# Depthwise convolution of a two-layer encoder: the taps that TensorE summed go to ScalarE and GpSimd

## The chip, the cores and the metric

The program runs on one core of a Trainium2 chip. A core has a matrix engine (TensorE, PE in the profile), a vector engine (VectorE, DVE), an activation engine (ScalarE, ACT), a general engine (GpSimd, POOL) and a queue engine (SyncE, SP). Each runs its own list of instructions in order; they meet at semaphores. SBUF is the working memory of 128 partitions, PSUM the memory that matmuls write, in eight banks of 512 float32 columns. The metric is the device time of one execution in microseconds (us), the median of several runs.

## The reference

Two layers of a streaming encoder over 384 tokens: one prompt of 256 and eight samples of 16. Layer 0 mixes by attention and retention, layer 1 by a convolution module; behind each stands a mixture of experts. What matters here is the convolution module, on 1024 channels, all float32:

```python
def conv_glu(h, w_pw1, b_pw1):
    a, g = jnp.split(jnp.einsum('btd,dc->btc', h, w_pw1) + b_pw1, 2, axis=-1)
    return a * jax.nn.sigmoid(g)

def conv_rest(u_ext, w_dw, b_dw, ln_g, ln_b, w_pw2):
    y = lax.conv_general_dilated(u_ext, w_dw[:, None, :], ... feature_group_count=CONV_CH) + b_dw
    y = jax.nn.silu(layer_norm(y, ln_g, ln_b))
    return jnp.einsum('btc,cd->btd', y, w_pw2)
```

`u_ext` is the gated projection with 30 tokens of history in front. Each channel's output is a sum of 31 shifted copies of its input, each times one weight of that channel (a tap).

## The kernel before

The channels lie on the partitions, in eight blocks c = 0 to 7 of 128 channels; a block has 384 token columns. The tile `U[:, c]` holds a block as 24 groups of 16 tokens, each with its 30 columns of history in front, so tap w of a block is one read of `U[:, c, :, w:w+16]`, 128x384.

The stage goes like this, all written out in order by hand, with semaphores between the engines:

- PE: `glu(c)` (L925 to L938) makes both halves of the projection of block c in two PSUM banks, with the weights in the slots that SP fills. `conv_taps(c)` (L940 to L949) then sums six taps in a third bank, as matmuls with diagonal matrices `DG`. The order is glu(0), then glu(c+1) and conv_taps(c) in turn (L951 to L955). Banks go round by three for GLU, by two for taps.
- ACT: `sigmoids(c)` (L1183) makes SGC; three copies (L1200 to L1202) spread the history over `U` and take the new sample tokens to `UN`; `diagonals(c+2)` (L1186) makes the six diagonal matrices of a later block.
- DVE: `gated(c)` (L1601) multiplies both halves of the GLU into `U`. Taps 6 to 30 follow, alternately summed in two accumulators, YC and YD (L1612 to L1626), with `gated(c+1)` between them, behind the fourteenth. L1630 adds YD to YC, L1632 adds PE's six taps from PSUM; then `y_conv` is signalled.
- POOL: nothing in this stage except, once, the stores of the convolution caches, when ACT has copied them out of PSUM (`ctok_ready`).

Behind it comes a tail for all blocks: PE sums the mean (L966), DVE centres (L1636), ACT squares (L1215), PE sums the variance (L970), ACT takes the root (L1217), DVE the reciprocal (L1639) and the product (L1642), ACT applies SiLU (L1221), and PE starts the second projection (L769). PE's transposes for the caches (L959, L961) stand ahead of the mean.

`q.do` and `q.link` are DVE's and ACT's helpers: they issue an instruction with a semaphore; `link` waits for it at once, `settle` for all that is open.

Of the kernel before, what the change touches and what calls it, by code (L numbers as in the profile page):

```python
# [19 lines left out]
ALU = mybir.AluOpType  # L20
ACT = mybir.ActivationFunctionType
AXX = mybir.AxisListType.X

P = 128
D = 1024
KD = D // P
NT = 3
TOK = NT * P
SEQ, NS, LS, PAST = 256, 8, 16, 128
# [9 lines left out]
CONV_W, HIST = 31, 30  # L39
# [10 lines left out]
NEG = -1e30  # L50
NBLK = TOK // LS
PBLK = SEQ // LS
PE_TAPS = 6
UNIT = 2048
LO, HI = 6, 12
NEAR = 6
# [108 lines left out]
def build(nc, a, o):  # L165

    with ExitStack() as ctx:
        sems = {}

        def S(name):  # L170
            if name not in sems:
                sems[name] = ctx.enter_context(nc.semaphore(name))
            return sems[name]
# [118 lines left out]
        NC = over("NC", [P, NT, D])  # L292
        YC = rc("YC", [P, KD, TOK])
        YD = rc("YD", [P, TOK])
        DG = rc("DG", [P, 2, PE_TAPS, P])
        VR = rc("VR", [P, TOK])
        SGC = rc("SGC", [P, 2, TOK])
        over = Region(rc.n, limit)
        UN = over("UN", [P, KD, P])
        CC = rc("CC", [P, 2, D])  # L300
        WDR = rc("WDR", [P, D])
        WDT = rc("WDT", [P, KD, CONV_W])
        SMR = rc("SMR", [P, P])
        SMT = rc("SMT", [P, 40])
        CS = WDR
        CP = rc("CP", [P, D])

        PS = nc.alloc_psum_tensor("PS", [P, 8, 512], F32)
# [134 lines left out]
        def _(pool):  # L443
# [41 lines left out]
            for lay in range(2):  # L485

                pool.wait_ge(S("x_mixed"), 8 * (lay + 1))
                pool.dma_start(WR[:, :, 0:NG], a["w_router_group"][lay].rearrange("(p k) n -> p k n", k=KD)
                               ).then_inc(S("router_in"), 16)
                pool.dma_start(WR[:, :, NG:NR], a["w_router_expert"][lay].rearrange("(p k) n -> p k n", k=KD)  # L490
                               ).then_inc(S("router_in"), 16)
                pool.dma_start(BR[:, 0:NG], row(a["b_router_group"][lay], NG)).then_inc(S("router_in"), 16)
                pool.dma_start(BR[:, NG:NR], row(a["b_router_expert"][lay], NE)).then_inc(S("router_in"), 16)
                if lay == 0:
                    pool.wait_ge(S("hn_ready"), 2 * NT)
                    pool.dma_start(gb[:, :], row(a["norm_mix"][1], D)).then_inc(S("gain_in"), 16)
                    pool.wait_ge(S("moe_done"), 1)
                    pool.dma_start(CC[0:120, 0, :], a["cache_conv"][0, 0:4].rearrange("b t c -> (b t) c")
                                   ).then_inc(S("conv_in"), 16)
                    pool.dma_start(CC[0:120, 1, :], a["cache_conv"][0, 4:8].rearrange("b t c -> (b t) c")  # L500
                                   ).then_inc(S("conv_in"), 16)
                    pool.dma_start(WDR[0:CONV_W, :], a["w_dw"][0]).then_inc(S("conv_in"), 16)
                    pool.dma_start(SMR[0:16, :], a["b_pw1"][0].rearrange("(c p) -> c p", p=P)
                                   ).then_inc(S("conv_in"), 16)
                    for i, name in enumerate(("b_dw", "conv_ln_g", "conv_ln_b")):
                        pool.dma_start(SMR[16 + 8 * i:24 + 8 * i, :], a[name][0].rearrange("(c p) -> c p", p=P)
                                       ).then_inc(S("conv_in"), 16)
                    pool.wait_ge(S("hn_ready"), 3 * NT)
                    pool.dma_start(gb[:, :], row(a["norm_ffn"][1], D)).then_inc(S("gain_in"), 16)

                    pool.wait_ge(S("ctok_ready"), 2)
                    store(o["conv_prompt"][0, 0], CP[0:HIST, :])
                    for b in range(NS):
                        store(o["conv_sample"][0, b, HIST - LS:HIST, :], CS[LS * b:LS * (b + 1), :])
                    pool.wait_ge(S("stored"), 16 * (STATE_STORES + CONV_STORES))
# [5 lines left out]
        def _(pe):  # L521
# [400 lines left out]
            pe.wait_ge(S("hn_ready"), 3 * NT)  # L922
            transpose_stream(NC)
            wait_stream(4)
            def glu(c):  # L925
                m, cc = divmod(c, 2)
                if cc == 0:
                    full("c", 2 * m)
                    full("c", 2 * m + 1)
                if c >= 3:  # L930
                    pe.wait_ge(S("u_ready"), c - 2)
                for g in range(2):
                    w = dense(2 * m + g)
                    for k in range(KD):
                        last = mm(PS[:, 2 * (c % 3) + g, 0:TOK], w[:, k, P * cc:P * (cc + 1)], HC[:, k, :],  # L935
                                  start=k == 0, stop=k == KD - 1)
                    if g == 1:
                        last.then_inc(S("glu_done"), 1)  # L938

            def conv_taps(c):  # L940

                pe.wait_ge(S("uhist_ready"), c + 1)
                pe.wait_ge(S("diag_ready"), PE_TAPS * (c + 1))
                if c >= 2:
                    pe.wait_ge(S("y_conv"), c - 1)
                for w in range(PE_TAPS):
                    last = mm(PS[:, 6 + c % 2, 0:TOK], DG[:, c % 2, w, :], U[:, c, :, w:w + LS],
                              start=w == 0, stop=w == PE_TAPS - 1)
                last.then_inc(S("pe_taps"), 1)  # L949

            glu(0)  # L951
            for c in range(KD):
                if c + 1 < KD:
                    glu(c + 1)
                conv_taps(c)  # L955

            pe.wait_ge(S("unew_ready"), KD)
            for c in range(KD):
                nc.tensor.transpose(PS[0:HIST, c // 4, P * (c % 4):P * (c % 4 + 1)], U[:, c, PBLK - 1, LS:LS + HIST],  # L959
# [3 lines left out]

            for c in range(KD):
                pe.wait_ge(S("y_conv"), c + 1)
                last = mm(PS[:, 4, 0:TOK], C["onesd"], YC[:, c, :], start=c == 0, stop=c == KD - 1)  # L966
            last.then_inc(S("mean_done"), 1)
            for c in range(KD):
                pe.wait_ge(S("ysq_ready"), c + 1)
                last = mm(PS[:, 5, 0:TOK], C["onesd"], YS[:, c, :], start=c == 0, stop=c == KD - 1)  # L970
            last.then_inc(S("var_done"), 1)
            pe.wait_ge(S("ctok_ready"), 2)
            project_out("c", 8, YC, "pw_done", 8, "z_ready")
# [5 lines left out]
        def _(act):  # L979
# [199 lines left out]
            def sigmoids(c):  # L1179
                act.wait_ge(S("glu_done"), c + 1)  # L1180
                if c >= 2:
                    act.wait_ge(S("u_ready"), c - 1)
                q.do(A(SGC[:, c % 2, :], PS[:, 2 * (c % 3) + 1, 0:TOK], ACT.Sigmoid, bias=SMT[:, 8 + c:9 + c]),  # L1183
                     S("sig_ready"))

            def diagonals(c):  # L1186

                if c >= 2:
                    act.wait_ge(S("pe_taps"), c - 1)
                for w in range(PE_TAPS):  # L1190
                    q.do(A(DG[:, c % 2, w, :], ident, ACT.Copy, scale=WDT[:, c, w:w + 1]), S("diag_ready"))

            act.wait_ge(S("hist_tr"), KD)
            diagonals(0)
            diagonals(1)
            sigmoids(0)
            for c in range(KD):

# [5 lines left out]
                q.settle()  # L1204
                if c + 1 < KD:
                    sigmoids(c + 1)
                if c + 2 < KD:
                    diagonals(c + 2)
            act.wait_ge(S("ctok_tr"), 1)
            q.do(A(CP[0:HIST, :], PS[0:HIST, 0:2, :].rearrange("p a n -> p (a n)"), ACT.Copy), S("ctok_ready"))  # L1210
            q.do(A(CS[:, :], PS[:, 2:4, :].rearrange("p a n -> p (a n)"), ACT.Copy), S("ctok_ready"))
# [2 lines left out]
                act.wait_ge(S("yc_centred"), c + 1)  # L1214
                q.do(A(YS[:, c, :], YC[:, c, :], ACT.Square), S("ysq_ready"))  # L1215
            act.wait_ge(S("var_done"), 1)
            q.link(A(VR[:, :], PS[:, 5, 0:TOK], ACT.Sqrt, bias=C["eps"]), S("cstd_ready"))  # L1217
            preload(ACT.Silu)
            for c in range(KD):
                act.wait_ge(S("yc_normed"), c + 1)  # L1220
# [6 lines left out]
        def _(dve):  # L1227
# [370 lines left out]
            def blocks(x):  # L1598
                return x.rearrange("p (b l) -> p b l", l=LS)

            def gated(c):  # L1601

                dve.wait_ge(S("sig_ready"), c + 1)
                q.do(V.scalar_tensor_tensor(U[:, c, :, HIST:], blocks(PS[:, 2 * (c % 3), 0:TOK]), SMT[:, c:c + 1],
                                            blocks(SGC[:, c % 2, :]), ALU.add, ALU.mult), S("u_ready"))

            gated(0)
            for c in range(KD):
                dve.wait_ge(S("uhist_ready"), c + 1)

                accs, sides = (blocks(YC[:, c, :]), blocks(YD[:, :])), (S("conv_a"), S("conv_b"))
                for w in range(PE_TAPS, CONV_W):  # L1612
                    n = w - PE_TAPS
                    acc, side = accs[n % 2], sides[n % 2]
                    if side is sides[1] and n < 2 and c:
                        dve.wait_ge(S("conv_sum"), c)
# [7 lines left out]
                    else:  # L1624
                        ins = V.scalar_tensor_tensor(acc, src, tap, acc, ALU.mult, ALU.add)  # L1625
                    q.do(ins, side)  # L1626
                    if n == 13 and c + 1 < KD:
                        gated(c + 1)
                q.settle()
                q.link(V.tensor_tensor(YC[:, c, :], YC[:, c, :], YD[:, :], ALU.add), S("conv_sum"))  # L1630
                dve.wait_ge(S("pe_taps"), c + 1)
                q.do(V.tensor_tensor(YC[:, c, :], YC[:, c, :], PS[:, 6 + c % 2, 0:TOK], ALU.add), S("y_conv"))  # L1632
            q.settle()
            dve.wait_ge(S("mean_done"), 1)
            for c in range(KD):
                q.do(V.tensor_tensor(YC[:, c, :], YC[:, c, :], PS[:, 4, 0:TOK], ALU.subtract), S("yc_centred"))  # L1636
            q.settle()
            dve.wait_ge(S("cstd_ready"), 1)
            q.link(V.reciprocal(VR[:, :], VR[:, :]))  # L1639
# [33 lines left out]
```

## Time and profile before

| | us |
|---|---|
| median of 3 runs (1300.19 to 1302.35) | 1300.33 |
| the profiled execution | 1300.19 |
| its span, first to last instruction | 1298.4 |
| busy in the span: PE | 1142.4 |
| DVE | 458.5 |
| ACT | 241.7 |
| POOL | 37.5 |

The span is what the profile covers; the time of the execution has 1.8 us more around it. A busy share is an average over stages: PE stands at 88% over the whole, while the convolution, from about 728 to 890 us of the span, has shares of its own.

How the rows are read. A row of a timeline gives the start in us from the span's start, the duration in us (from the first start to the last end, if it merges several), engine, line, operation, output and inputs, the count, and in brackets how long the engine was idle before and who released it. A row of the instruction groups gives the shape and count, then the busy us in total and the mean ns of one, then the idle time before them. A row of the waits gives engine, tile and line, what it waited for, and us in total, times and longest. A row of the windows gives the stretch, its length, then for PE, PEld (weight load), DVE, ACT and POOL the busy us with the number of instructions, then the granted TensorE clock as a share of 2.4 GHz, the busy share of the DMA engines and GB/s.

### The profile page before, as it was taken

Reading aid. Unit: us, or ns where it says so; the run is one execution under the profiler, and the core shown is the slowest. Engines: PE = TensorE matmul, PEld = TensorE weight load, DVE = VectorE, ACT = ScalarE, POOL = GpSimd, SP = SyncE. Lnnn points to the kernel's source line nnn. Section 1 sums busy time; section 2 is a strip of 40 time slices with the busy share of each in tenths; the row PEclk is TensorE's granted clock in tenths of the full one; section 3 lists DMA queues with packets and bytes.
Section 4 is the critical chain, followed back from the end, with each engine's and each line's share of the span. In section 5 each row is a group of like instructions: output and inputs, shape, how many; then the busy total and the mean of one; then the engine's idle time right before and its main releaser. Section 6 shows DMA issues by size and latency. Waiting matters only on the chain. (4 is left out here: it accounts for less than half of the span.)

```text
span 1298.4 us, 15664 instructions
## 1 busy us (share of the span) xinstructions
PE 1142.4 (88%) x6307; PEld 843.0 (65%) x6307; DVE 458.5 (35%) x869; ACT 241.7 (19%) x502; POOL 37.5 (3%) x64
## 2 busy tenths in 40 slices
PE   3998895789579999999996899959759999999996
PEld 2887794568566766766663555528657666776673
DVE  1122335450422333123322499970431332133323
ACT  2005323320211111111112322131211111111110
POOL 2000000010100000000001000010000000000000
PEclk9989997569769999999998899979769999999999
DMA  9422214227108878778784123701207878787761
GB/s 274 149 65 90 65 66 171 74 61 282 54 1 346 327 284 337 276 307 325 279 313 134 34 68 107 279 20 65 70 1 323 318 272 338 298 321 289 297 258 49
DMA packets 71528, 249.48 MB, mean 192 GB/s; under 512 B 4779, under 2 KB 33571, under 8 KB 54960
## 3 DMA queue, kind: packets, MB, share of 16 engines
q1 hardware_dynamic: 68224, 239.42, 49.0%
q0 software_dynamic: 3264, 9.51, 2.8%
q8 instruction: 27, 0.44, 0.1%
q14 instruction: 13, 0.11, 0.0%
HBM read 243.93 MB, written 5.44 MB: 192 GB/s over the span
## 5 line engine op out<-in xcount | busy, mean ns | idle before, releaser
L815 PE MATMUL PS<-slot,XG 128*64 128x256 f32 x2048 | 229.0, 382 | 2.4 <-ACT XG L1125 2.4
L815 PEld LDWEIGHTS PS<-slot,XG 128*64 128x64 f32 x2048 | 146.9, 138 | 83.0 <-issue 13.7
L805 PE MATMUL PS<-G,XHI 128*128 128x256 f32 x384 | 159.6, 416 | 11.2 <-DVE G L1535 8.9
L805 PE MATMUL PS<-G,XLO 128*128 128x256 f32 x384 | 156.1, 406 | 0.0
L805 PEld LDWEIGHTS PS<-G,XHI 128*128 128x128 f32 x384 | 129.1, 336 | 11.8 <-DVE G L1535 9.2
L1570 DVE SCALAR_TENSOR_TENSOR YL<-PS,GATE,YH 128x1024 fp32r<-128x1024 f32 x32 | 41.1, 1284 | 270.0 <-ACT YH L1145 270.0
L565 PE MATMUL PS<-slot,HT 128*128 128x256 f32 x576 | 131.7, 388 | 2.9 <-ACT PJ L1014 2.2
L805 PEld LDWEIGHTS PS<-G,XLO 128*128 128x128 f32 x384 | 130.0, 338 | 0.0
L565 PEld LDWEIGHTS PS<-slot,HT 128*128 128x128 f32 x576 | 110.9, 195 | 18.9 <-issue 2.9
L838 PE MATMUL PS<-slot,HID 128*64 128x512 f32 x512 | 116.9, 598 | 6.1 <-issue 4.8
L1577 DVE TENSOR_TENSOR X<-X,PS 128x512 f32<-128x512 f32 x96 | 66.0, 687 | 104.7 <-PE PS L885 104.7
L885 PE MATMUL PS<-YH,GT 128*128 128x512 f32 x192 | 82.2, 428 | 5.7 <-DVE YL L1570 5.7
L935 PE MATMUL PS<-HC,slot 128*128 128x384 f32 x256 | 83.8, 486 | 0.7 <-ACT HC L1002 0.7
L885 PE MATMUL PS<-YL,GT 128*128 128x512 f32 x192 | 77.1, 402 | 0.0
L838 PEld LDWEIGHTS PS<-slot,HID 128*64 128x64 f32 x512 | 34.7, 136 | 64.6 <-issue 61.0
L935 PEld LDWEIGHTS PS<-HC,slot 128*128 128x128 f32 x256 | 48.5, 190 | 34.8 <-issue 1.9
L1137 ACT ACTIVATE SG<-PS 128x256 f32<-128x256 f32 x32 | 12.3, 384 | 312.0 <-PE PS L815 312.0
L1125 ACT ACTIVATE XG<-PS 128x1024 f32<-128x1024 f32 x32 | 32.8, 1025 | 178.9 <-PE PS L805 178.9
L1550 DVE TENSOR_TENSOR hid_by_token<-PS,SG 128x256 f32<-128x256 f32 x32 | 13.5, 422 | 129.6 <-ACT SG L1137 129.6
L1625 DVE SCALAR_TENSOR_TENSOR YC<-U,WDT,YC 128x384 f32<-128x384 f32 x96 | 58.8, 613 | 0.0
L885 PEld LDWEIGHTS PS<-YH,GT 128*128 128x128 f32 x192 | 37.0, 193 | 32.0 <-DVE X L1577 13.1
L1625 DVE SCALAR_TENSOR_TENSOR YD<-U,WDT,YD 128x384 f32<-128x384 f32 x88 | 53.9, 613 | 0.0
(324 smaller groups left out, 1127.3 us busy)
## 6 DMA issues: line engine op xcount, KB each, us to landing
slot<-in_w_exp_gate SPq DMA_DIRECT2D x64, 1024.0 KB, 6.7
slot<-in_w_exp_up SPq DMA_DIRECT2D x64, 1024.0 KB, 8.0
slot<-in_w_exp_down SPq DMA_DIRECT2D x64, 1024.0 KB, 7.0
slot<-in_w_in_mix SPq DMA_DIRECT2D x12, 1024.0 KB, 9.3
slot<-in_w_pw SPq DMA_DIRECT2D x12, 1024.0 KB, 7.7
slot<-in_w_out_mix SPq DMA_DIRECT2D x4, 1024.0 KB, 10.8
slot<-in_cache_fox_k SPq DMA_DIRECT2D x2, 1024.0 KB, 5.4
slot<-in_cache_fox_v SPq DMA_DIRECT2D x2, 1024.0 KB, 5.3
```

The source lines that it names most:

```text
L565: last = mm(PS[:, b0 + t // 2, UCOL * (t % 2):UCOL * (t % 2) + UCOL], HT[:, k, P * t:P * (t + 1)], w[:, k, :], start=k == 0, stop=k == KD - 1)
L805: last = mm(out, v, G[:, QUAD * t:QUAD * (t + 1), :], start=t + part == 0, stop=t + part == NT)
L815: last = mm(PS[CAP * e:CAP * (e + 1), 2 + pair, FE * gu:FE * (gu + 1)], XG[:, k, CAP * (2 * pair + e):CAP * (2 * pair + e + 1)], w[:, k, : ...
L838: last = mm(PS[CAP * e:CAP * (e + 1), 4 + n, :], HID[:, pair, j, e, :], w[:, j, 512 * n:512 * (n + 1)], start=j == 0, stop=j == 1, skip_gr ...
L885: last = mm(PS[:, 6 + i % 2, :], GT[:, pair, P * t:P * (t + 1)], y[:, pair, 512 * n:512 * (n + 1)], start=pair + part == 0, stop=pair + pa ...
L935: last = mm(PS[:, 2 * (c % 3) + g, 0:TOK], w[:, k, P * cc:P * (cc + 1)], HC[:, k, :], start=k == 0, stop=k == KD - 1)
L1125: q2 = A(XG[:, 4 * half:4 * half + 4, :].rearrange("p k n -> p (k n)"), PS[:, 0:2, :].rearrange("p a n -> p (a n)"), ACT.Copy)
L1137: A(SG[:, pair, :], PS[:, 2 + pair, 0:FE], ACT.Silu).then_inc(S("silu_ready"), 1)
L1550: V.tensor_tensor(HT2[:, pair, :], PS[:, 2 + pair, FE:2 * FE], SG[:, pair, :], ALU.mult).then_inc(S("hid_ready"), 1)
L1570: V.scalar_tensor_tensor(YL[:, pair, :], PS[:, 4:6, :].rearrange("p a n -> p (a n)"), GATE[:, pair:pair + 1], YH[:, pair, :].bitcast(F32), ...
L1577: V.tensor_tensor(v, v, PS[:, 6 + i % 2, :], ALU.add).then_inc(S("x_added"), 1)
L1625: ins = V.scalar_tensor_tensor(acc, src, tap, acc, ALU.mult, ALU.add)
```

## The change

PE no longer takes taps: `conv_taps` and `diagonals` are gone, and GLU uses four pairs of banks in turn. Taps 0 to 10 of each block are made by ACT as products (an activation with the tap as scale): tap 0 goes to the accumulator YP, taps 1 to 10 go by turns to two buffers PR, and POOL adds each into YP. ACT may be at most two products ahead of POOL (`pool_tap`, n - 2), and POOL waits for each add before the next. DVE keeps 20 taps, 11 to 30, and its last sum reads YP in SBUF. DVE's `gated(c+1)` stands ahead of the taps of block c. The cache rows CS get a tile of their own.

```diff
-PE_TAPS = 6
+POOL_TAPS = 11
...
+        PR = over("PR", [P, 2, TOK])
...
-        CS = WDR
+        CS = rc("CS", [P, D])
...
+                    for c in range(KD):
+                        acc = YP[:, c % 2, :]
+                        pool.wait_ge(S("first_product"), c + 1)
+                        for w in range(1, POOL_TAPS):
+                            n = c * (POOL_TAPS - 1) + w
+                            pool.wait_ge(S("product_ready"), n)
+                            if n > 1:
+                                pool.wait_ge(S("pool_tap"), n - 1)
+                            nc.gpsimd.tensor_tensor(acc, acc, PR[:, (n - 1) % 2, :], ALU.add).then_inc(S("pool_tap"), 1)
                     pool.wait_ge(S("ctok_ready"), 2)
...
-            glu(0)
-            for c in range(KD):
-                if c + 1 < KD:
-                    glu(c + 1)
-                conv_taps(c)
-
+            pe.wait_ge(S("uhist_ready"), KD)
             pe.wait_ge(S("unew_ready"), KD)
...
                 q.settle()
                 if c + 1 < KD:
                     sigmoids(c + 1)
-                if c + 2 < KD:
-                    diagonals(c + 2)
+
+                if c >= 2:
+                    act.wait_ge(S("y_conv"), c - 1)
+                for w in range(POOL_TAPS):
+                    n = c * (POOL_TAPS - 1) + w
+                    if w and n > 2:
+                        act.wait_ge(S("pool_tap"), n - 2)
+                    dst = (PR[:, (n - 1) % 2, :] if w else YP[:, c % 2, :]).rearrange("p (b l) -> p b l", l=LS)
+                    q.do(A(dst, U[:, c, :, w:w + LS], ACT.Copy, scale=WDT[:, c, w:w + 1]),
+                         S("product_ready" if w else "first_product"))
...
             gated(0)
             for c in range(KD):
+                if c + 1 < KD:
+                    gated(c + 1)
                 dve.wait_ge(S("uhist_ready"), c + 1)
...
-                for w in range(PE_TAPS, CONV_W):
-                    n = w - PE_TAPS
+                for w in range(POOL_TAPS, CONV_W):
+                    n = w - POOL_TAPS
...
-                    if n == 13 and c + 1 < KD:
-                        gated(c + 1)
...
-                dve.wait_ge(S("pe_taps"), c + 1)
-                q.do(V.tensor_tensor(YC[:, c, :], YC[:, c, :], PS[:, 6 + c % 2, 0:TOK], ALU.add), S("y_conv"))
+                dve.wait_ge(S("pool_tap"), (c + 1) * (POOL_TAPS - 1))
+                q.do(V.tensor_tensor(YC[:, c, :], YC[:, c, :], YP[:, c % 2, :], ALU.add), S("y_conv"))
```

DVE, at the start of the stage, before. `U<-PS,SMT,SGC` is `gated`, `YC<-U,WDT,SMT` the first tap of a block on this engine:

```order
L1259 COPY HC<-PS 128x384 x4
L1604 SCALAR_TENSOR_TENSOR U<-PS,SMT,SGC 128x24x16
L1621 TENSOR_SCALAR YC<-U,WDT,SMT 128x384
L1623 TENSOR_SCALAR YD<-U,WDT 128x384
L1625 SCALAR_TENSOR_TENSOR YC<-U,WDT,YC 128x384
L1625 SCALAR_TENSOR_TENSOR YD<-U,WDT,YD 128x384
```

DVE at the same place, after:

```order
L1252 COPY HC<-PS 128x384 x4
L1597 SCALAR_TENSOR_TENSOR U<-PS,SMT,SGC 128x24x16 x2
L1616 TENSOR_SCALAR YC<-U,WDT,SMT 128x384
L1618 TENSOR_SCALAR YD<-U,WDT 128x384
L1620 SCALAR_TENSOR_TENSOR YC<-U,WDT,YC 128x384
L1620 SCALAR_TENSOR_TENSOR YD<-U,WDT,YD 128x384
```

The second `gated` now stands ahead of the first tap. ACT, the same start, before, from the copies of the normed tokens to the third block; `DG` are the diagonals, `SGC` the sigmoids:

```order
L1002 ACTIVATE HC<-PS 128x384 x4
L1191 ACTIVATE DG<-cst,WDT 128x128 x12
L1183 ACT_TABLE_LOAD
L1183 ACTIVATE SGC<-PS,SMT 128x384
L1200 ACTIVATE U<-U 128x15x16
L1201 ACTIVATE U<-U 128x14x14
L1202 ACTIVATE UN<-U 128x128
L1183 ACTIVATE SGC<-PS,SMT 128x384
L1191 ACTIVATE DG<-cst,WDT 128x128 x6
L1200 ACTIVATE U<-U 128x15x16
```

ACT at the same place, after:

```order
L996 ACTIVATE HC<-PS 128x384 x4
L1177 ACT_TABLE_LOAD
L1177 ACTIVATE SGC<-PS,SMT 128x384
L1185 ACTIVATE U<-U 128x15x16
L1186 ACTIVATE U<-U 128x14x14
L1187 ACTIVATE UN<-U 128x128
L1177 ACTIVATE SGC<-PS,SMT 128x384
L1200 ACTIVATE YP<-U,WDT 128x384
L1200 ACTIVATE PR<-U,WDT 128x384 x10
L1185 ACTIVATE U<-U 128x15x16
```

Where six diagonals stood, eleven products stand, and the copies for the next block follow them. POOL after, between its last load and its first store:

```order
L510 DMA gain_rows<-in_norm_ffn 128x1024
L520 ISA
L520 TENSOR_TENSOR YP<-YP,PR 128x384 x80
L456 DMA out_conv_prompt<-CP 30x1024
L456 DMA out_conv_sample<-CS 16x1024 x8
```

The 80 adds stand ahead of the stores of the caches; before, the load of the gain row and the stores stood one behind the other.

## Rows read from the trace of the kernel before

**Rows 1.** Windows, all engines, second `gated` to the end of the last sum:
```profile
749.93:859.13 109.20, 99.33 (x315) 57.71 (x313) 108.20 (x209) 23.46 (x67) 4.35 (x9) 0.97 0.41 141
```

**Rows 2.** Timeline, DVE, convolution blocks:
```profile
740.44 0.48 DVE L1621 TENSOR_SCALAR YC<-U,WDT,SMT 128x384 f32<-128x384 f32 x1 [0.73 <-ACT U L1201]
...
749.40 0.62 DVE L1604 SCALAR_TENSOR_TENSOR U<-PS,SMT,SGC 128x384 f32<-128x384 f32 x1 [1.79 <-ACT SGC L1183]
...
756.99 0.47 DVE L1621 TENSOR_SCALAR YC<-U,WDT,SMT 128x384 f32<-128x384 f32 x1
...
757.71 0.61 DVE L1625 SCALAR_TENSOR_TENSOR YC<-U,WDT,YC 128x384 f32<-128x384 f32 x1
758.24 0.61 DVE L1625 SCALAR_TENSOR_TENSOR YD<-U,WDT,YD 128x384 f32<-128x384 f32 x1
...
771.65 0.47 DVE L1621 TENSOR_SCALAR YC<-U,WDT,SMT 128x384 f32<-128x384 f32 x1
...
858.58 0.55 DVE L1632 TENSOR_TENSOR YC<-YC,PS 128x384 f32<-128x384 f32 x1
```

**Rows 3.** Timeline, PE matmuls, GLU (L935) and taps (L947):
```profile
727.79 20.88 PE L935 MATMUL PS<-HC,slot 128*128 128x384 f32 x64 [0.70 <-ACT HC L1002]
...
752.53 10.48 PE L935 MATMUL PS<-HC,slot 128*128 128x384 f32 x32
762.85 4.19 PE L947 MATMUL PS<-U,DG 128*128 128x384 f32 x12
766.88 10.48 PE L935 MATMUL PS<-HC,slot 128*128 128x384 f32 x32
```

**Rows 4.** Waits, 735 to 860:
```profile
DVE U L1604 <- ACT SGC L1183: 13.2, 2, 11.4
...
PE PS L966 <- DVE YC L1632: 9.9, 1, 9.9
```

**Rows 5.** Groups of instructions by line, 735 to 860:
```profile
L1625 DVE SCALAR_TENSOR_TENSOR YC<-U,WDT,YC 128x384 f32<-128x384 f32 x96 | 58.8, 613 | 0.0
...
L947 PE MATMUL PS<-U,DG 128*128 128x384 f32 x96 | 33.6, 499 | 0.0
...
L1630 DVE TENSOR_TENSOR YC<-YC,YD 128x384 f32<-128x384 f32 x8 | 4.5, 558 | 0.7
L1632 DVE TENSOR_TENSOR YC<-YC,PS 128x384 f32<-128x384 f32 x8 | 4.4, 553 | 0.3
...
L1623 DVE TENSOR_SCALAR YD<-U,WDT 128x384 f32<-128x384 f32 x8 | 3.3, 415 | 0.0
```

**Rows 6.** Windows of the tail:
```profile
862.00:870.00 8.00, 7.83 (x16) 4.16 (x16) 2.75 (x6) 3.31 (x8) 0.00 (x0) 0.68 0.00 0
...
875.00:880.00 5.00, 5.00 (x12) 3.94 (x13) 2.15 (x5) 4.98 (x8) 0.00 (x0) 0.50 0.00 0
```

**Rows 7.** Timeline, ACT and the POOL issue that waits for it:
```profile
748.78 0.58 ACT L1183 ACTIVATE SGC<-PS,SMT 128x384 f32<-128x384 f32 x1 [8.18 <-PE PS L935]
...
754.50 0.39 ACT L1200 ACTIVATE U<-U 128x240 f32<-128x240 f32 x1
...
755.06 0.29 ACT L1202 ACTIVATE UN<-U 128x128 f32<-128x128 f32 x1
...
845.78 1.00 ACT L1211 ACTIVATE WDR<-PS 128x1024 f32<-128x1024 f32 x1
...
847.07 0.52 POOL L455 DMA_DIRECT2D out_conv_prompt<-CP  x1 [128.37 <-ACT WDR L1211]
...
861.60 3.71 ACT L1215 ACTIVATE YS<-YC 128x384 f32<-128x384 f32 x8 [13.30 <-DVE YC L1636]
```

**Rows 8.** Groups of instructions by line, POOL, whole span:
```profile
L476 POOL MEMSET VM<- 128x2048 f32 x1 | 1.8, 1823 | 0.0
...
L1664 POOL MEMSET const-float32-0.0<- 128x1 f32 x1 | 0.1, 98 | 0.3 <-issue 0.3
```

**Rows 9.** Groups of instructions by line, DVE, 230 to 245, a PSUM source:
```profile
L1374 DVE COPY PT<-PS 128x384 f32<-128x384 f32 x2 | 1.1, 557 | 0.7 <-PE PS L696 0.7
```

More of the change, by code:

```diff
@@ L294, in build @@
         YD = rc("YD", [P, TOK])
-        DG = rc("DG", [P, 2, PE_TAPS, P])
+        YP = rc("YP", [P, 2, TOK])
         VR = rc("VR", [P, TOK])
@@ L924, in _ @@
             wait_stream(4)
-            def glu(c):
+            for c in range(KD):
                 m, cc = divmod(c, 2)
@@ L929, in glu @@
                     full("c", 2 * m + 1)
-                if c >= 3:
-                    pe.wait_ge(S("u_ready"), c - 2)
+                if c >= 4:
+                    pe.wait_ge(S("u_ready"), c - 3)
                 for g in range(2):
@@ L934, in glu @@
                     for k in range(KD):
-                        last = mm(PS[:, 2 * (c % 3) + g, 0:TOK], w[:, k, P * cc:P * (cc + 1)], HC[:, k, :],
+                        last = mm(PS[:, 2 * (c % 4) + g, 0:TOK], w[:, k, P * cc:P * (cc + 1)], HC[:, k, :],
                                   start=k == 0, stop=k == KD - 1)
@@ L938, in glu @@
                         last.then_inc(S("glu_done"), 1)
[L940 to L949, printed above, removed]
-            glu(0)
-            for c in range(KD):
-                if c + 1 < KD:
-                    glu(c + 1)
-                conv_taps(c)
+            pe.wait_ge(S("uhist_ready"), KD)
             pe.wait_ge(S("unew_ready"), KD)
@@ L965, in _ @@
                 pe.wait_ge(S("y_conv"), c + 1)
-                last = mm(PS[:, 4, 0:TOK], C["onesd"], YC[:, c, :], start=c == 0, stop=c == KD - 1)
+                last = mm(PS[:, 6, 0:TOK], C["onesd"], YC[:, c, :], start=c == 0, stop=c == KD - 1)
             last.then_inc(S("mean_done"), 1)
@@ L969, in _ @@
                 pe.wait_ge(S("ysq_ready"), c + 1)
-                last = mm(PS[:, 5, 0:TOK], C["onesd"], YS[:, c, :], start=c == 0, stop=c == KD - 1)
+                last = mm(PS[:, 7, 0:TOK], C["onesd"], YS[:, c, :], start=c == 0, stop=c == KD - 1)
             last.then_inc(S("var_done"), 1)
@@ L1182, in sigmoids @@
                     act.wait_ge(S("u_ready"), c - 1)
-                q.do(A(SGC[:, c % 2, :], PS[:, 2 * (c % 3) + 1, 0:TOK], ACT.Sigmoid, bias=SMT[:, 8 + c:9 + c]),
+                q.do(A(SGC[:, c % 2, :], PS[:, 2 * (c % 4) + 1, 0:TOK], ACT.Sigmoid, bias=SMT[:, 8 + c:9 + c]),
                      S("sig_ready"))
[L1186 to L1191, printed above, removed]
             act.wait_ge(S("hist_tr"), KD)
-            diagonals(0)
-            diagonals(1)
             sigmoids(0)
@@ L1216, in _ @@
             act.wait_ge(S("var_done"), 1)
-            q.link(A(VR[:, :], PS[:, 5, 0:TOK], ACT.Sqrt, bias=C["eps"]), S("cstd_ready"))
+            q.link(A(VR[:, :], PS[:, 7, 0:TOK], ACT.Sqrt, bias=C["eps"]), S("cstd_ready"))
             preload(ACT.Silu)
@@ L1603, in gated @@
                 dve.wait_ge(S("sig_ready"), c + 1)
-                q.do(V.scalar_tensor_tensor(U[:, c, :, HIST:], blocks(PS[:, 2 * (c % 3), 0:TOK]), SMT[:, c:c + 1],
+                q.do(V.scalar_tensor_tensor(U[:, c, :, HIST:], blocks(PS[:, 2 * (c % 4), 0:TOK]), SMT[:, c:c + 1],
                                             blocks(SGC[:, c % 2, :]), ALU.add, ALU.mult), S("u_ready"))
@@ L1635, in _ @@
             for c in range(KD):
-                q.do(V.tensor_tensor(YC[:, c, :], YC[:, c, :], PS[:, 4, 0:TOK], ALU.subtract), S("yc_centred"))
+                q.do(V.tensor_tensor(YC[:, c, :], YC[:, c, :], PS[:, 6, 0:TOK], ALU.subtract), S("yc_centred"))
             q.settle()
```

## The prediction

> **What bounds the kernel now.** I read the page first, then the windows of the convolution stage, then the groups of instructions by line, the waits and the timeline there. The window [rows 1] covers the 109.2 us from the second `gated` to the last convolution sum: VectorE (DVE) is busy for 108.2 of them. TensorE (PE) looks busy as well, 99.3 us, so it must be asked which of the two leads. The timeline answers. One channel block on DVE takes 771.65 - 756.99 = 14.66 us, and the following ones repeat it [rows 2]. On PE a block of GLU and six taps takes 766.88 - 752.53 = 14.35 us [rows 3], a little less, and after its last matmul PE waits 9.9 us for DVE's last sum YC; DVE itself waits for nothing after its second `gated` [rows 4]. So DVE leads by 0.3 us a block, with PE right behind: whoever relieves only one of the two gains almost nothing. The change relieves both.
>
> **DVE, part by part.** A DVE tap starts 0.53 us after the one before (757.71, 758.24), though it lasts 0.61 [rows 2, 5]. Five taps per block go, 25 down to 20: 5 x 0.53 = 2.65 us, so a block takes 14.66 - 2.65 = 12.01 us. The last sum reads YP in place of PSUM; 0.56 against 0.55 us for the same width [rows 5], nothing. `gated(c+1)` moves from the middle of block c to its front. For blocks after the first that costs nothing as long as GLU is ahead: PE now needs 762.85 - 752.53 = 10.3 us a column [rows 3], less than 12. For the first block it costs a lot: `gated(1)` needs GLU column 1 and its sigmoid, so it still starts at 749.40, and all taps of block 0 now stand behind it, where the first tap started at 740.44 before [rows 2]. DVE therefore begins at 749.93. Blocks 0 and 7 carry no `gated` in this count (12.01 - 0.53 = 11.48), six do: 2 x 11.48 + 6 x 12.01 = 95.0, end at 749.9 + 95.0 + 0.1 = 845.0. Before, the last sum ended at 858.58 + 0.55 = 859.1 [rows 2]. Left to itself DVE would finish 14.1 us sooner.
>
> **PE** loses 96 tap matmuls, 33.6 us busy [rows 5]. It ends its GLU near 728 + 8 x 10.3 = 811 and then waits for DVE. Worth nothing beyond what DVE shows. The tail runs at the lower of the two clock levels in part already (granted 0.50 at 875 to 880, 0.68 while the 16 variance matmuls take 7.83 us) [rows 6]. If all 16 ran at 1.2 GHz they would take at most 7.83 x 0.68 / 0.50 = 10.6; I count 0 and keep 2.8 us as an upper end.
>
> **ScalarE (ACT)** loses the diagonals and gets eleven products of 128x384 per block. The nearest row is the Square of the same shape, 3.71 us for eight, 0.46 each [rows 7]: 5.1 us a block, plus a sigmoid (from 748.78 to `gated(1)` at 749.40, 0.62 with the hand-over [rows 2, 7]) and three copies in 0.85 (754.50 to 755.35) [rows 7]: 6.6 of 12 us. ACT is not the bound. Its order matters, though: per block copies, sigmoid, products; the last products are paced by POOL, and only then do copies for the next block begin. The table load now stands behind the wait for GLU 0 and moves later with it, hidden because `gated(1)` is 10 us away. The two 1.0 us copies of the cache rows now come after the last product, with a table load behind them; they take about 3.5 us, while the last one or two adds, the two sums, the mean and the centring take longer than that. Nothing.
>
> **POOL (GpSimd)** gets 80 adds of 128x384, ten per block, each reading two tensors in SBUF and each waiting for the one before. The trace has no POOL instruction that reads SBUF, only memsets and DMA issues. Bounds: the memset of 2048 columns took 1.823 us, the one of one column 0.098, so 0.84 ns a column, 0.324 us for 384 [rows 8]. The lower end is a write alone, 0.098 + 0.324 = 0.42 us. The upper end is three passes, two reads and the write one after another: 0.098 + 0.97 = 1.07. I take the middle of two and three passes, 0.81 + 0.098 = 0.91 us. From the Trainium skill, GPSIMD Engine Reference, section "Performance versus the Vector engine": 2048 columns of a two-input add took 4497 ns there at about 2.6 cycles each, which would make an estimate of 0.89 us here; no run here shows it.
>
> **Do DVE and POOL read side by side?** This decides the sign. DVE's own rows say that it has a second way into SBUF: a one-input operation from SBUF takes 0.415 us, a copy of the same 384 columns from PSUM 0.557, the two-input tap 0.613 [rows 5, 9]. The one-input form reads faster than a column per step, and a two-input form must use that second way for its second tensor. Nothing shows that POOL has a way of its own, and 20 of the 23 instructions of a DVE block now (18 taps and two sums) are such two-input operations, nearly without a gap. POOL's memset [rows 8] proves nothing on it, as it reads no SBUF tensor. I forecast that they take turns. The Trainium skill, SBUF — State Buffer, section "SBUF: two separate sides", says the pair of ports shared by the two is "an exclusive lock, not a bandwidth split", for a whole instruction, taken also by a DVE operation with two SBUF inputs against a GpSimd one that reads SBUF. By that rule the sum is the one that follows, without it the 14 us above; the measured rows here are only compatible with it.
>
> With turns, the order does not matter, only the sum: what POOL holds is added to DVE's chain, since each block's last sum waits for POOL's ten adds. Per add 0.91 us, and 0.08 because DVE's taps, normally overlapped (0.61 long, 0.53 apart), lose that at each turn: 0.99 x 80 = 79.2. End 845.0 + 79.2 = 924.2 in place of 859.1, **+65.1 us**. The profiled execution took 1300.19 us (span 1298.4), the median is 1300.33, so 1300.2 + 65.1 = **1365**. The ends: 0.42 x 80 = 34 gives 845 + 34 - 859 = +20, 1320. With 1.07 + 0.08 and POOL's answer to a semaphore (0.29 us, from an ACT copy's end at 845.78 + 1.00 to 847.07 [rows 7]) covered by nothing, 1.44 x 80 = 115 gives +101, 1401.
>
> **The rivals.**
> 1. *Side by side, POOL quick enough (faster).* Speaks for it: DVE drops 2.65 us and PE 4 us a block, both chains shrink. POOL's own loop: from the last product, three copies 0.85, settling 0.1, sigmoid 0.6, two products 0.9, POOL's answer 0.3, so 2.8; then eight adds until the last product may go, and 0.6 for it: 3.4 + 8p, where p is an add with its wait. With p = 1.1 that is 12.2 against DVE's 12.0: POOL starts near 750.6, ends at 750.6 + 11 + 7 x 12.2 = 847, and with the last sum 847.9: -11, so 1289. With p under 1.07 DVE leads, -14, 1286.
> 2. *Side by side, POOL's chain too slow.* p = 1.07 + 0.3 = 1.37 gives 14.4 a block: 750.6 + 13.7 + 100.8 + 0.9 = 866, +7, 1307. It turns from gain to loss at p near 1.28. Against it: 0.3 was read after long waits; for it: the adds form one serial chain.
> 3. *POOL is starved by DVE until DVE reaches its wait.* The adds then run alone, each with POOL's answer of up to 0.29 us: 12.0 + 10 x (0.91 + 0.29) = 24.0 a block, times eight less the two missing `gated` 191, end 941, 1382. I count it with the forecast, in whose range it lies.
>
> **How the numbers follow.** Turns 0.69; rival 1 0.17; rival 2 0.14, of which most is slower. Slower than before by over 0.2% (2.6 us, about what a measurement of this kernel can tell from no change): 0.69 + 0.11 = 0.80; within it 0.03; faster 0.17. The forecast's own range is 1320 to 1401. The range given reaches down to take in rival 2 and leaves rival 1: 1298 to 1400.
>
> **What would show it.** In the profile after: DVE taps or POOL adds longer than alone. Forecast: POOL adds well over 1 us beside DVE, or DVE taps with gaps; block period 21 to 23 us; last YC sum near 924; PE idle for about 110 us of the stage. Rival 1: taps still 0.53 apart and adds under 1.1 us, period 12. Rival 2: taps 0.53 apart, DVE's idle time in front of the YP sum, on POOL. First TENSOR_SCALAR of YC near 749.9 in every case. My forecast is wrong if the taps keep 0.53 while POOL's adds run.

## The result: slower by 3.3%, because the two engines take turns

The changed kernel takes 1343.37 us (median of 4 runs, 1342.7 to 1344.31), the kernel before 1300.26 us (median of 4 runs). The ratio is 1.033, 95% interval 1.0314 to 1.0346. The forecast was 1365 with turns between VectorE (DVE) and GpSimd (POOL); the sign and the cause are right, and the loss of 43 us is two thirds of the 65 forecast. By turns I mean that an instruction of the one engine, though started, doesn't get on until most of the other's is done.

The window of the changed kernel from the first tap of block 0 to the end of the last sum (columns as before: PE, weight load, DVE, ACT, POOL busy, then the clock, DMA share, GB/s):

```profile
749.08:901.63 152.55, 70.21 (x219) 41.31 (x217) 151.21 (x183) 64.71 (x118) 115.42 (x89) 0.73 0.29 101
```

DVE is still busy all the time, 151.2 of 152.6 us, but with 183 instructions where 209 took 108.2 in [rows 1]; and that window leaves out the first fourteen taps of block 0, which stood ahead of the second `gated` then, while this one has all taps. It does less work in more time. PE is busy for less than half of the stretch. The groups by line, changed kernel, say which instructions grew:

```profile
L1620 DVE SCALAR_TENSOR_TENSOR YC<-U,WDT,YC 128x384 f32<-128x384 f32 x72 | 67.7, 940 | 0.0
L1625 DVE TENSOR_TENSOR YC<-YC,YP 128x384 f32<-128x384 f32 x8 | 7.2, 897 | 0.3
L1618 DVE TENSOR_SCALAR YD<-U,WDT 128x384 f32<-128x384 f32 x8 | 5.7, 713 | 0.0
L1597 DVE SCALAR_TENSOR_TENSOR U<-PS,SMT,SGC 128x384 f32<-128x384 f32 x8 | 4.9, 610 | 21.1 <-ACT SGC L1177 21.1
L520 POOL TENSOR_TENSOR YP<-YP,PR 128x384 f32<-128x384 f32 x80 | 111.0, 1388 | 65.1 <-ACT PR L1200 54.8
```

The tap of two SBUF inputs went from 613 to 940 ns on average against [rows 5]; `gated`, the same operation with one input in PSUM, stayed at 610. Both stand in the same stream on the same engine. The TENSOR_SCALAR of YD, with one input, grew too, from 415 to 713. The row of `gated` in the groups of the kernel before:

```profile
L1604 DVE SCALAR_TENSOR_TENSOR U<-PS,SMT,SGC 128x384 f32<-128x384 f32 x8 | 4.9, 614 | 13.2 <-ACT SGC L1183 13.2
```

The timeline of block 0, changed kernel, shows the turns one by one:

```profile
748.55 0.62 DVE L1597 SCALAR_TENSOR_TENSOR U<-PS,SMT,SGC 128x384 f32<-128x384 f32 x1 [8.32 <-ACT SGC L1177]
749.08 0.47 DVE L1616 TENSOR_SCALAR YC<-U,WDT,SMT 128x384 f32<-128x384 f32 x1
749.70 12.48 POOL L520 TENSOR_TENSOR YP<-YP,PR 128x384 f32<-128x384 f32 x10 [32.24 <-ACT PR L1200]
749.80 1.35 DVE L1620 SCALAR_TENSOR_TENSOR YC<-U,WDT,YC 128x384 f32<-128x384 f32 x1
751.08 1.35 DVE L1620 SCALAR_TENSOR_TENSOR YD<-U,WDT,YD 128x384 f32<-128x384 f32 x1
752.35 1.35 DVE L1620 SCALAR_TENSOR_TENSOR YC<-U,WDT,YC 128x384 f32<-128x384 f32 x1
```

While POOL makes its ten adds, a DVE tap starts every 1.27 us instead of every 0.53 us: each add costs DVE 0.74 us. I call this price of an add the hold. The first TENSOR_SCALAR stands at 749.08, 22.1 us after PE's first GLU matmul (726.94); 749.93, where the prediction has DVE begin, lies as far behind the first GLU matmul of [rows 3]. The distance from that matmul to the end of the last sum grew from 131.3 (727.79 to 859.13) to 174.7 us, by 43.4, the whole of the loss. What comes behind the last sum takes 438.6 us to the end of the span, 439.3 before: the tail is unchanged.

### The profile page after: what moved, and what is told of

Its sections match the earlier page's. It is cut to its first block and busy times, and to the rows that moved or that the text cites. A ratio compares the mean times of both kernels' runs of the same rounds, so it can differ in the third digit from the quotient of the medians.

```text
span 1340.2 us, 15634 instructions
## 1 busy us (share of the span) xinstructions
PE 1112.1 (83%) x6211; PEld 824.8 (62%) x6211; DVE 494.4 (37%) x829; ACT 279.8 (21%) x542; POOL 148.5 (11%) x144
## 5 line engine op out<-in xcount | busy, mean ns | idle before, releaser
L1563 DVE SCALAR_TENSOR_TENSOR YL<-PS,GATE,YH 128x1024 fp32r<-128x1024 f32 x32 | 41.1, 1284 | 272.4 <-ACT YH L1139 272.4
L520 POOL TENSOR_TENSOR YP<-YP,PR 128x384 f32<-128x384 f32 x80 | 111.0, 1388 | 65.1 <-ACT PR L1200 54.8
L1620 DVE SCALAR_TENSOR_TENSOR YD<-U,WDT,YD 128x384 f32<-128x384 f32 x72 | 68.4, 950 | 0.0
L1620 DVE SCALAR_TENSOR_TENSOR YC<-U,WDT,YC 128x384 f32<-128x384 f32 x72 | 67.7, 940 | 0.0
L1200 ACT ACTIVATE PR<-U,WDT 128x384 f32<-128x384 f32 x80 | 49.4, 628 | 63.0 <-POOL YP L520 63.0
```

Of the source, the lines that this page charges most:

```text
L520: nc.gpsimd.tensor_tensor(acc, acc, PR[:, (n - 1) % 2, :], ALU.add).then_inc(S("pool_tap"), 1)
L1200: q.do(A(dst, U[:, c, :, w:w + LS], ACT.Copy, scale=WDT[:, c, w:w + 1]), S("product_ready" if w else "first_product"))
L1563: V.scalar_tensor_tensor(YL[:, pair, :], PS[:, 4:6, :].rearrange("p a n -> p (a n)"), GATE[:, pair:pair + 1], YH[:, pair, :].bitcast(F32), ...
```

## The experiments

Seven kernels. Each is compared with the kernel before on the same chip, whose median there was 1300.39 us (first four) and 1301.81 us (last three). For comparison within the stage I use one distance throughout: from the first GLU matmul to the end of the last convolution sum. Before it is 131.3 us, changed kernel 174.7.

**Accumulators in PSUM.** No DVE tap has two SBUF inputs any more. GLU goes round by three pairs of banks, to leave two for the accumulators.

```diff
-                accs = (blocks(YC[:, c, :]), blocks(YD[:, :]))
+                accs = (blocks(PS[:, 6, 0:TOK]), blocks(PS[:, 7, 0:TOK]))
...
+                q.link(V.tensor_tensor(YC[:, c, :], YP[:, c % 2, :], PS[:, 6, 0:TOK], ALU.add), S("conv_sum"))
+                q.do(V.tensor_tensor(YC[:, c, :], YC[:, c, :], PS[:, 7, 0:TOK], ALU.add), S("y_conv"))
```

> The changed kernel, but DVE keeps both accumulators in PSUM banks 6 and 7 (GLU goes round by three bank pairs again), and its two last sums read one tensor from PSUM each, so no DVE tap has two SBUF inputs. Turns theory (a DVE instruction with two SBUF inputs and a POOL add exclude each other): the taps stay 0.53 us apart beside POOL's adds, the adds take about 1 us each, the block period is about 12, the last convolution sum ends near 845 to 850 instead of 901.6, time 1286 to 1292. Rival (ACT's eleven products a block, or POOL's traffic as such, slow every SBUF access of DVE): ACT and POOL do the same work here, so the time stays within 10 us of 1343.

Measured: 1292.02 us, ratio 0.9928 (0.9902 to 0.9955); distance 852.2 - 730.2 = 122.0 us. Timeline of this kernel, block 0 and the start of block 1:

```profile
752.37 0.68 DVE L1616 TENSOR_SCALAR PS<-U,WDT,SMT 128x384 f32<-128x384 f32 x1
752.99 11.29 POOL L520 TENSOR_TENSOR YP<-YP,PR 128x384 f32<-128x384 f32 x10 [32.47 <-ACT PR L1200]
753.48 9.54 DVE L1620 SCALAR_TENSOR_TENSOR PS<-U,WDT,PS 128x384 f32<-128x384 f32 x18
764.41 0.55 DVE L1624 TENSOR_TENSOR YC<-YP,PS 128x384 f32<-128x384 f32 x1 [1.40 <-POOL YP L520]
765.41 11.29 POOL L520 TENSOR_TENSOR YP<-YP,PR 128x384 f32<-128x384 f32 x10 [1.13 <-ACT PR L1200]
765.48 0.61 DVE L1597 SCALAR_TENSOR_TENSOR U<-PS,SMT,SGC 128x384 f32<-128x384 f32 x1
766.00 0.67 DVE L1616 TENSOR_SCALAR PS<-U,WDT,SMT 128x384 f32<-128x384 f32 x1
...
778.47 0.67 DVE L1616 TENSOR_SCALAR PS<-U,WDT,SMT 128x384 f32<-128x384 f32 x1
790.92 0.67 DVE L1616 TENSOR_SCALAR PS<-U,WDT,SMT 128x384 f32<-128x384 f32 x1
```

Eighteen taps in 9.54 us, 0.53 apart, beside ten adds in 11.29. ACT makes the same products, POOL the same adds on the same tensors; for DVE's taps only the place of the accumulator has changed. The rival, that ACT's or POOL's traffic slows DVE as such, is out. The taps now also write PSUM in place of SBUF, so this run alone doesn't tell the second input from the write. `gated` does: it writes SBUF, beside an add at 765.48, and takes 0.61 us as before. This also gives the price of an add without DVE in the way: 0.999 us busy (79.9 us for 80), a new one about every 1.14 us. The two TENSOR_SCALAR cost more when they write PSUM, 0.67 and 0.61 against 0.47 and 0.42, 0.4 us a block together, so a block takes 12.45 us and not 12.0. The time lies at the upper end of the 1286 to 1292 expected, and the last sum ends at 852.2, not at 845 to 850.

**POOL only writes.** A memset in place of the add; the products are left out of the sum.

```diff
-                            nc.gpsimd.tensor_tensor(acc, acc, PR[:, (n - 1) % 2, :], ALU.add)
+                            nc.gpsimd.memset(acc, 0.0)
```

> The changed kernel, but each of POOL's 80 adds is a memset of YP, 128x384: it writes and reads nothing, so the products are left out of the sum. Turns theory in the form that only reading is exclusive: the taps go back to 0.53 us, DVE ends near 844 + 1, time about 1286. If any SBUF access of POOL excludes DVE's two-input operations: each memset (0.42 us alone) is added, 80 x 0.4 = 32, time about 1318. Rival (ACT's products slow DVE): taps stay stretched, time near 1343.

Measured: 1284.35 us (one run), distance 844.3 - 725.9 = 118.4 us. Timeline, start of block 1:

```profile
759.06 0.95 POOL L520 MEMSET YP<- 128x384 f32 x2 [4.66 <-ACT PR L1200]
759.14 0.56 DVE L1625 TENSOR_TENSOR YC<-YC,YP 128x384 f32<-128x384 f32 x1
759.62 0.61 DVE L1597 SCALAR_TENSOR_TENSOR U<-PS,SMT,SGC 128x384 f32<-128x384 f32 x1
760.14 0.70 DVE L1616 TENSOR_SCALAR YC<-U,WDT,SMT 128x384 f32<-128x384 f32 x1
760.21 0.99 POOL L520 MEMSET YP<- 128x384 f32 x2 [0.20 <-ACT PR L1200]
760.76 0.65 DVE L1618 TENSOR_SCALAR YD<-U,WDT 128x384 f32<-128x384 f32 x1
761.33 0.60 DVE L1620 SCALAR_TENSOR_TENSOR YC<-U,WDT,YC 128x384 f32<-128x384 f32 x1
761.86 0.60 DVE L1620 SCALAR_TENSOR_TENSOR YD<-U,WDT,YD 128x384 f32<-128x384 f32 x1
```

Two-input taps and sums run at full speed beside a writing POOL (taps 607 ns on average, 0.53 apart). So it is POOL's reading that they take turns with. The fast one-input TENSOR_SCALAR does meet the memsets: 0.70 and 0.65 here, 0.47 and 0.42 alone.

**POOL with one input.** A copy of PR to YP; the sum is left out.

```diff
-                            nc.gpsimd.tensor_tensor(acc, acc, PR[:, (n - 1) % 2, :], ALU.add)
+                            nc.gpsimd.tensor_copy(acc, PR[:, (n - 1) % 2, :])
```

> The changed kernel, but each of POOL's adds is a copy of PR to YP, one SBUF input instead of two, so the sum is left out. Turns theory: still turns, the hold is shorter, one reading pass of about 0.32 us and the start, so 0.4 to 0.5 instead of 0.72 us a time: DVE ends at 844 + 32 to 40, time 1318 to 1327. If only two-input operations of POOL exclude DVE: 1286.

Measured: 1303.95 us (one run), distance 862.8 - 726.7 = 136.1 us. Timeline, block 0:

```profile
749.49 6.75 POOL L520 COPY YP<-PR 128x384 f32<-128x384 f32 x9 [32.34 <-ACT PR L1200]
749.59 0.86 DVE L1620 SCALAR_TENSOR_TENSOR YC<-U,WDT,YC 128x384 f32<-128x384 f32 x1
750.37 0.85 DVE L1620 SCALAR_TENSOR_TENSOR YD<-U,WDT,YD 128x384 f32<-128x384 f32 x1
751.15 0.85 DVE L1620 SCALAR_TENSOR_TENSOR YC<-U,WDT,YC 128x384 f32<-128x384 f32 x1
```

There are turns, but each costs only 0.78 - 0.53 = 0.25 us, not the 0.4 to 0.5 expected: my pricing of a hold by passes was too dear. One input holds 0.25, two inputs 0.74: for the same columns the second input triples it. Over the whole, the distance is 136.1 - 118.4 = 17.7 us longer than with memsets, 0.22 a copy.

**Six taps.** POOL_TAPS 6 in place of 11, so 40 adds and 25 DVE taps a block.

> The changed kernel with 6 taps on ACT and POOL in place of 11: 40 adds instead of 80, 25 DVE taps a block instead of 20. Turns theory with 0.53 us a DVE tap and 0.72 us held per add: 40 x 0.53 = 21.2 us more and 40 x 0.72 = 28.8 us less, so 7.6 us faster than the changed kernel, 1336. Rival (POOL's own chain sets the end, so half of its adds give half of the loss back and the DVE taps are hidden): about 1310 or less.

Measured: 1335.4 us, ratio 1.026 (1.0234 to 1.0287); 8.0 less than the changed kernel, distance 897.4 - 730.7 = 166.6, 8.1 less. 7.6 was expected, and the rival's 1310 is out. The exchange rate holds: a tap given to POOL spares DVE 0.53 us and costs it about 0.73, as 40 x (0.73 - 0.53) = 8.

**Accumulators in PSUM and `gated` in the middle.** As the first experiment, with the order of before restored.

```diff
-                if c + 1 < KD:
-                    sigmoids(c + 1)
                 for w in range(POOL_TAPS):
+                    if w == 6 and c + 1 < KD:
+                        sigmoids(c + 1)
...
-                if c + 1 < KD:
-                    gated(c + 1)
                 dve.wait_ge(S("uhist_ready"), c + 1)
...
+                    if n == 15 and c + 1 < KD:
+                        gated(c + 1)
```

> Accumulators in PSUM as in the run before, and the order of before restored: gated(c+1) stands in the middle of DVE's taps of block c (behind the sixteenth), and ACT makes sigmoid(c+1) ahead of product 6 of block c. If the front position of gated cost the delay that the prediction counted (first tap 8 to 9 us later), DVE starts near 14 us after GLU's first matmul instead of 22, everything behind it follows: 1292 - 8 = 1284, down to 1281 as POOL's restart loses the sigmoid (0.6 us a block, where POOL leads). Rival (GLU, 10.35 us a column and first ready 10.4 us in, becomes the bound as soon as DVE starts early): gated stalls in the first blocks, gain under 4 us, 1288 or more.

Measured: 1285.36 us (6 runs), ratio 0.9864 (0.9837 to 0.9892), faster than both kernels, and 1.4 us above the 1284 expected; distance 843.8 - 728.5 = 115.3 us, 6.7 less than with `gated` in front. Timeline, starts of the first blocks:

```profile
742.48 0.68 DVE L1613 TENSOR_SCALAR PS<-U,WDT,SMT 128x384 f32<-128x384 f32 x1 [0.73 <-ACT U L1186]
...
756.26 0.56 DVE L1623 TENSOR_TENSOR YC<-YP,PS 128x384 f32<-128x384 f32 x1 [2.60 <-POOL YP L520]
...
757.32 0.68 DVE L1613 TENSOR_SCALAR PS<-U,WDT,SMT 128x384 f32<-128x384 f32 x1
...
769.73 0.68 DVE L1613 TENSOR_SCALAR PS<-U,WDT,SMT 128x384 f32<-128x384 f32 x1
```

DVE's first tap now stands 14.0 us behind the first GLU matmul, not 22.1. Of these 8.1 us, two amounts go back in block 0. DVE waits 2.6 us there for POOL, where it waited 1.4 with `gated` in front; POOL's sixth add starts 0.9 us late, since its product stands behind the sigmoid and that waits for GLU. And `gated(1)`, 0.5 us, now lies behind the first tap. That leaves 8.1 - 1.2 - 0.5 = 6.4 of the 6.7 measured. After that a block takes 12.4 us. GLU doesn't stop DVE itself after `gated(0)`.

**The same order with accumulators in SBUF.** The same diff on the changed kernel.

> The changed kernel (accumulators in SBUF) with gated(c+1) in the middle of the taps and sigmoid(c+1) ahead of product 6. Turns theory: the sum of DVE work and 80 holds of 0.72 us is the same, only the start is 8.2 us earlier: 1343 - 8 = 1335. If the loss of the changed kernel came from the order (the start delay and the starved adds) rather than from turns, it would fall back to 1300 or less.

Measured: 1340.03 us, ratio 1.0288 (1.0249 to 1.0326), distance 898.3 - 728.4 = 169.8. The order is not the cause of the loss: the distance is 4.9 us shorter than in the changed kernel. The time is 3.3 us lower, but the intervals of the two ratios overlap (the changed kernel's is 1.0314 to 1.0346), so the times alone don't show a gain. 8 was expected, a miss. Timeline, two block starts:

```profile
762.63 1.15 DVE L1613 TENSOR_SCALAR YC<-U,WDT,SMT 128x384 f32<-128x384 f32 x1
...
782.19 1.15 DVE L1613 TENSOR_SCALAR YC<-U,WDT,SMT 128x384 f32<-128x384 f32 x1
```

A block takes 19.56 us, that is 12.01 + 10 x 0.755: every add finds a DVE instruction to hold up, the one-input TENSOR_SCALAR too, 1.15 us in place of 0.47. In the changed kernel the mean over all 80 was 0.72. The difference, 80 x 0.035 = 2.8 us, and the 0.5 of `gated(1)`, which now lies behind the first tap, are the missing gain: 8.1 - 2.8 - 0.5 = 4.8. Some of the adds that passed free in the changed kernel can be named: `gated` stands beside an add three times there (at 774.58, 807.53 and 845.82) and takes 0.60 us each time; in this run no add runs beside it.

**One accumulator in PSUM, one in SBUF.** As the first experiment, but the second accumulator, and with it one input of the last sum, is YD in SBUF.

```diff
-                accs = (blocks(PS[:, 6, 0:TOK]), blocks(PS[:, 7, 0:TOK]))
+                accs = (blocks(PS[:, 6, 0:TOK]), blocks(YD[:, :]))
```

> As the PSUM run, but only accumulator A is in PSUM; accumulator B is in SBUF, so of DVE's taps every second one has two SBUF inputs. Turns theory: a POOL add holds 0.74 us and can pass 0.53 of it beside the PSUM tap, so a pair of taps takes 0.53 + 0.74 = 1.27 us instead of 1.06 (both free) or 2 x 1.27 (both in turn); 9 pairs a block, 8 blocks: 9 x 8 x 0.21 = 15 us more than the PSUM run's 1292, about 1307. If holds simply add whenever such taps are in the chain: half or all of 59 us more, 1320 to 1350.

Measured: 1311.81 us (one run), distance 869.7 - 729.2 = 140.5, 18.5 over the first experiment. Timeline, block 0:

```profile
753.51 0.61 DVE L1620 SCALAR_TENSOR_TENSOR PS<-U,WDT,PS 128x384 f32<-128x384 f32 x1
754.04 0.83 DVE L1620 SCALAR_TENSOR_TENSOR YD<-U,WDT,YD 128x384 f32<-128x384 f32 x1
754.79 0.61 DVE L1620 SCALAR_TENSOR_TENSOR PS<-U,WDT,PS 128x384 f32<-128x384 f32 x1
755.31 0.83 DVE L1620 SCALAR_TENSOR_TENSOR YD<-U,WDT,YD 128x384 f32<-128x384 f32 x1
```

A pair takes 1.28 us, 0.53 + 0.74 as expected: the PSUM tap runs inside POOL's hold, the SBUF tap waits for the rest of it. The 3.5 us above the 15 expected lie in the second tap of each block, which writes YD fast from one SBUF input: it takes 1.013 us on average here, 0.610 in the first experiment, 8 x 0.4 = 3.2.

## Why the prediction was right, and where its size was off

- *DVE leads, PE right behind.* Right: with POOL out of the way and PE relieved, the stage shrank by 9 to 16 us in three experiments. That whoever relieves only one of the two gains almost nothing, no run tested.
- *Turns between two-input DVE operations and POOL's adds.* Right, and now shown from both sides: the PSUM accumulators remove the loss while POOL works on, the memsets remove it while DVE's taps stay as they are. The prediction counted 20 of the 23 instructions of a block as open to it; it is 22, since both TENSOR_SCALAR with source and target in SBUF take turns with an add as well (1.15 and up to 1.22 us against 0.47 and 0.42). The Trainium skill, SBUF — State Buffer, section "SBUF: two separate sides", has an exclusive lock between a DVE operation with two SBUF inputs and a GpSimd operation that reads SBUF, for the whole instruction. These runs agree on who meets whom, but not on the whole instruction: an add of 0.999 us and a tap whose distance alone is 0.53 share a period of 1.27 us, so they overlap by about a quarter of a microsecond.
- *What a turn costs.* This is the term that was mis-sized: 0.91 + 0.08 = 0.99 us an add, 79 us. Measured (152.55 - 95.0) / 80 = 0.72, 57.5 us. The step that missed is "what POOL holds is added to DVE's chain" with the whole instruction put for the hold. The instruction itself was priced well, 0.91 against 0.999; a quarter of it lies beside DVE's tap, and the 0.08 for lost overlap is already inside the measured 0.74, since both distances are from start to start. With 0.72 the prediction's own sum gives 845.0 + 57.5 - 859.1 = +43.4. That it comes out is no test, as 0.72 is what the stage leaves when 95.0 is taken off. The tests are the single turns (0.74), the exchange rate with six taps (0.73) and the even blocks with `gated` in the middle (0.755). The estimate from the figures of the Trainium skill, GPSIMD Engine Reference, section "Performance versus the Vector engine", was 0.89 us for the instruction; the run without turns has 0.999.
- *The late start.* Right in place: the first tap is 22.1 us behind the first GLU matmul. The experiment with the old order makes it 14.0; in a stage without turns that was worth 6.7 us, not the full 8.1.
- *The order of turns does not matter.* Right but for the 2.8 us that the even blocks cost more (0.755 against 0.72 an add), though the order was not as I drew it. POOL ran one block ahead, as YP has two buffers, and in some blocks it was kept waiting (starved). The timeline of POOL, changed kernel:

```profile
749.70 12.48 POOL L520 TENSOR_TENSOR YP<-YP,PR 128x384 f32<-128x384 f32 x10 [32.24 <-ACT PR L1200]
763.07 12.45 POOL L520 TENSOR_TENSOR YP<-YP,PR 128x384 f32<-128x384 f32 x10 [0.88 <-ACT PR L1200]
778.10 12.90 POOL L520 TENSOR_TENSOR YP<-YP,PR 128x384 f32<-128x384 f32 x10 [2.59 <-ACT PR L1200]
797.74 19.34 POOL L520 TENSOR_TENSOR YP<-YP,PR 128x384 f32<-128x384 f32 x10 [6.74 <-ACT PR L1200]
```

  Ten adds take 12.5 us in turns (1.27 each, where they need 1.14 alone); the ten at 797.74 take 19.3, since the first of them is open for 8.2 us while DVE runs its taps 0.53 apart without a gap. It is done only when DVE has come to its first sum (805.20).
- *Rivals.* Rival 1 (side by side, faster) is what happens once the accumulators lie in PSUM: 12.45 us a block and 1292 us. Rival 2 (POOL's chain too slow by itself) is out: p, an add with its wait, is 1.14, under the turning point of 1.28 that the prediction gave. Rival 3 (POOL starved until DVE waits) came true in part only: in some blocks POOL was kept out for 8.2 us, but its adds then took turns with DVE and did not run alone, so a block took 19.1 us on average and not 24.0.
- *The signs named.* The adds are well over 1 us (1.39 on average) and DVE's taps have turns, as forecast. The sizes follow the cheaper turn: block 19.1 us, not 21 to 23; last sum ending at 901.6, not 924; PE idle for 82 us in the window shown, not 110.
- *ACT, the tail, the PE clock.* Nothing that shows, as forecast. ACT's product was priced too low, 0.46 against 0.61 to 0.63 us, but ACT spends 63.0 us of the stage waiting for POOL. The granted clock from the last sum on is 0.77 over 30 us, 0.76 before.

## What to carry to other kernels

Before elementwise work goes from DVE to POOL, look at what DVE runs meanwhile: against DVE operations with two SBUF inputs, a two-input POOL operation takes more from DVE (0.72 us here) than the tap it removes (0.53). Put one of DVE's operands in PSUM and the two engines do run side by side; that turned a loss of 3.3% into a gain of 0.7%, and of 1.4% with `gated` back in the middle. And an instruction moved ahead of a loop moves the first wait of the stage with it: count the start, not only the period.

## What the runs showed of the hardware that I had not expected

- A POOL add costs DVE less than its own length: 0.74 us of 0.999 for two inputs of 384 columns. A POOL copy, one input of 384 columns, costs 0.25.
- One-input DVE operations aren't safe either: a TENSOR_SCALAR from SBUF to SBUF went from 0.42 to 1.22 us beside an add. Written to PSUM it took 0.61 to 0.67, beside adds too.
- A writing POOL does not touch two-input DVE operations, but slows the fast one-input form from 0.47 to 0.70 us.
- DVE instructions that follow each other without a gap can keep POOL out for a whole run of taps: one add stood open for 8.2 us. At other times (778.10) an add got in after one tap of an equally dense row; what decides it is not shown.
